# FFN-up by Strassen's scheme: seven block products in place of eight in a two-layer decoder step

## The reference

```python
def swiglu(h, w1, w3, w2):
    return (jax.nn.silu(h @ w1) * (h @ w3)) @ w2

h = rmsnorm(x, w['norm_ffn1'])
x = x + 0.5 * swiglu(h, w['ffn1_w1'], w['ffn1_w3'], w['ffn1_w2'])
...
x = x + m @ w['w_o']
h = rmsnorm(x, w['norm_ffn2'])
x = x + 0.5 * swiglu(h, w['ffn2_w1'], w['ffn2_w3'], w['ffn2_w2'])
gate = jax.nn.sigmoid(rmsnorm(x, w['norm_ple']) @ w['w_ple_gate'])
x = x + gate * (ple.astype(x.dtype) @ w['w_ple'])
```

## Time and profile before

| | |
|---|---|
| median of 3 runs | 2717.16 us (2717.04 to 2717.97) |
| span of the profiled execution | 2715.9 us (no other time of it is given) |
| TensorE busy | 2679.2 us, 99% |
| DVE, ACT, POOL busy | 1353.4, 1028.2, 241.3 us |
| matmuls | 23860 |
| read from HBM | 290.30 MB |

### The profile page before, as it was taken

How to read it: one execution, slowest core, us unless ns; L and a number is a source line. 1 busy time by engine, 2 the same in 40 slices (tenths; PEclk the granted TensorE clock), 3 DMA queues, 4 the chain that set the end, 5 groups by cost and what they waited for, 6 DMA issues and landing times.

```text
span 2715.9 us, 56484 instructions
## 1 busy us (share of the span) xinstructions
PE 2679.2 (99%) x23860; PEld 2545.4 (94%) x23860; DVE 1353.4 (50%) x1708; ACT 1028.2 (38%) x1184; POOL 241.3 (9%) x150
## 2 busy tenths in 40 slices
PE   8999999999999999999999999999999999999997
PEld 8999999976699999999999999999757999999997
DVE  5333338665666533333643333467466755333336
ACT  5333223423653433332343332333246624333223
POOL 0111000331000011100001100012310000111000
PEclk9999999999999999999999999999999999999998
DMA  4222232178422222222322222322873222222221
GB/s 149 92 93 78 96 128 95 66 239 283 146 93 94 92 90 90 84 82 90 109 94 93 92 72 94 125 93 87 282 259 120 78 94 94 93 93 78 86 100 63
DMA packets 119536, 303.81 MB, mean 112 GB/s; under 512 B 14947, under 2 KB 25187, under 8 KB 118883
## 3 DMA queue, kind: packets, MB, share of 16 engines
q1 hardware_dynamic: 119394, 301.79, 32.5%
HBM read 290.30 MB, written 11.44 MB: 111 GB/s over the span
## 4 chain that ended last, share of the span: by engine, by line
PE 94%; DVE 3%; DVEq 1%; ACT 1%; issue 0%; DMA 0%; SPq 0%; POOLq 0%; ACTq 0%
PE ps L620 70%; PE ps L668 13%; PE ps L835 2%; PE ps L927 1%; PE ps L990 1%; PE ps L975 1%; PE ps L716 1%; PE ps L946 1%; PE ps L721 1%; PE ps L1144 1%; DVEq L1819 0%; PE ps L1004 0%; DVE sc L2031 0%; PE ps L1036 0%; PE ps L1008 0%
## 5 line engine op out<-in xcount | busy, mean ns | idle before, releaser
L620 PE MATMUL ps<-Hh,whi 128*128 128x260 f32 x3440 | 692.6, 283 | 11.9 <-DVE Hl L1745 10.4
L1246 ACT ACTIVATE whi<-raw 128x2048 fp32r<-128x2048 f32 (+2 forms) x225 | 396.0, 1760 | 780.1 <-PE ps L620 670.9
L620 PE MATMUL ps<-Hl,whi 128*128 128x260 f32 x3440 | 690.7, 282 | 0.0
L620 PE MATMUL ps<-Hh,wlo 128*128 128x260 f32 x3440 | 689.7, 282 | 0.0
L1679 DVE TENSOR_TENSOR wlo<-raw,whi 128x2048 fp32r<-128x2048 f32 (+2 forms) x213 | 444.2, 2085 | 291.9 <-ACT whi L1246 291.7
L620 PEld LDWEIGHTS ps<-Hh,whi 128*128 128x128 f32 x3440 | 528.7, 188 | 13.1 <-issue 11.3
L620 PEld LDWEIGHTS ps<-Hl,whi 128*128 128x128 f32 x3440 | 530.9, 189 | 0.0
L620 PEld LDWEIGHTS ps<-Hh,wlo 128*128 128x128 f32 x3440 | 530.0, 189 | 0.0
L1246 ACT ACT_TABLE_LOAD x163 | 209.1, 1283 | 305.8 <-PE ps L620 233.5
L1679 DVE TENSOR_TENSOR ta<-ps,R 128x520 f32<-128x520 f32 x88 | 61.6, 700 | 475.9 <-PE ps L620 474.7
L620 PE MATMUL ps<-Gh,whi 128*128 128x260 f32 x1408 | 283.7, 283 | 0.0
(11 more groups left out here) (288 smaller groups left out, 2899.2 us busy)
## 6 DMA issues: line engine op xcount, KB each, us to landing
raw<-in_ffn_up SPq DMA_DIRECT2D x176, 512.0 KB, 4.3
raw<-in_ffn_down SPq DMA_DIRECT2D x128, 352.0 KB, 3.1
kb<-in_cache_k SPq DMA_DIRECT2D x128, 256.0 KB, 3.9
kb<-in_cache_v SPq DMA_DIRECT2D x128, 256.0 KB, 4.0
raw<-in_w_in SPq DMA_DIRECT2D x56, 512.0 KB, 4.4
raw<-in_w_gate SPq DMA_DIRECT2D x32, 512.0 KB, 4.5
raw<-in_w_ab SPq DMA_DIRECT2D x16, 512.0 KB, 4.3
raw<-in_w_o SPq DMA_DIRECT2D x16, 512.0 KB, 4.2
```

What stands on the lines that cost most here:

```text
L620: last = nc.tensor.matmul(ps[:, bank + 2 * m + c, 0:HT], w, x[:, k0 + k, c * HT:(c + 1) * HT], start=starts and k == 0 and n == 0, stop=st ...
L1246: return nc.scalar.activation(out, in_, func, **kw)
```

## The change

The product [X0 X1] by [w1 w3] is seen as a 2 x 2 block product: the tokens in two halves, the channels in even and odd chunks, the columns as w1 and w3. Strassen's scheme (in Winograd's form) makes it of seven products in place of eight, from sums of blocks of weights and sums of blocks of activations.

- Weights: of the four quarters of a block (512 columns each) POOL makes three more by four subtractions (`up_sums`, one of them a step on the way to another). ACT and DVE split seven quarters in three groups, UHa/ULa in two halves and UHb/ULb.
- Activations: `pair_act` and `pair_dve` take two chunks at a time: two scaled copies, four sums of 260 columns on DVE, and the split of seven parts into HA and HB. Of block 0 the first three products may run on a pair as it becomes ready, the others wait for all four pairs.
- TensorE: `up_block` runs seven products of 4 x 3 matmuls, each into one bank. Products 4 and 7 add into the bank of product 1, product 5 into that of product 2; ACT copies the bank's content out before each. DVE adds the copy to the bank when the block is done, and then multiplies by R.
- FFN-down goes over two groups of four output chunks, first half of the rows and then second half for each.
- The FFN loops of DVE, ACT, POOL and SP are written out; buffers are laid out anew; the low parts of G of the first ten blocks are made within the loop, two blocks later, the other twelve behind it.

The core of the diff (`HT` is 260; `WF` are two raw buffers, weven and wodd, and weven_71, wodd_66 in the order are their second parts):

```diff
-            def ffn(L, nb, up, down, first=0):
-                with sp_.Fori(first, KF // 2) as i:
-                    for p in range(2):
-                        load(L, nb + 2 * i + p, p, dyn(up, L, 2 * i + p))
-                with sp_.Fori(0, KD) as i:
-                    for hf in range(2):
-                        load(L, nb + KF + 2 * i + hf, hf, dyn(down, L, 2 * i + hf), cols=11 * P)
+            def ffn(L, nb, up, down, hid):
+                for n in range(KF):
+                    if n == 1:
+                        sp_.wait_ge(block_done, L * NB + nb + FREE)
+                    else:
+                        sp_.wait_ge(split_done, L * NB + nb + (n or 1) + 1)
+                    for q in range(2):
+                        sp_.dma_start(WF[n % 2][q][:, 0:3:2, :],
+                                      up[L, n][:, 1024 * q:1024 * (q + 1)].rearrange("p (a c) -> p a c", a=2)
+                                      ).then_inc(raw_ready[n % 2], 16)
+                for n in range(2 * KD):
+                    sp_.wait_ge(split_done, L * NB + nb + KF + (n if n > 1 else 0) + 1)
+                    if n == 1:
+                        sp_.wait_ge(up_sum, 4 * (up_first(L, hid) + KF) - 3)
+                    for a0 in (0, 11 * P // 2):
+                        sp_.dma_start(rawd[n % 2][:, a0:a0 + 11 * P // 2], down[L, n][:, a0:a0 + 11 * P // 2]
+                                      ).then_inc(raw_ready[n % 2], 16)
+                    if hid and n == 1:
+                        sp_.wait_ge(split_done, L * NB + nb + KF + FREE)
+                        sp_.dma_start(PT[:, :, :], A["p"][L]).then_inc(p_load, 16)
...
+            BANK = (2, 3, 1, 2, 3, 0, 2)
+
+            def up_waits(L, nb, ub, nj, hid, n, p, f):
+                g = up_first(L, hid)
+                if f == 0:
+                    pe.wait_ge(up_lo, 2 * n + (2 * g + 1))
+                    pe.wait_ge(evac, L * NE + n + (ub + 1))
+                elif f == 2:
+                    pe.wait_ge(up_lo, 2 * n + (2 * g + 2))
+                elif f == 4:
+                    pe.wait_ge(split_done, n + (L * NB + nb + FREE + 1))
+                if f in (3, 4, 6):
+                    pe.wait_ge(up_copy, 4 * n + (4 * g + {3: 1, 4: 2, 6: 3}[f]))
+
+            def up_product(p, f, i0=0, i1=4, before=None):
+                for i in range(i0, i1):
+                    if before:
+                        before(i)
+                    w = slice(i * P, (i + 1) * P)
+                    for t, (a, x) in enumerate(((WH[f], XH[f]), (WH[f], XL[f]), (WL[f], XH[f]))):
+                        last = nc.tensor.matmul(ps[:, 4 * p + BANK[f], 0:HT], a[:, w], x[:, i, :],
+                                                start=f in (0, 1, 2, 5) and i == 0 and t == 0, stop=i == 3 and t == 2,
+                                                skip_group_check=True)
+                if i1 == 4:
+                    last.then_inc(block_done if f == 6 else up_form, 1)
+
+            def up_block(L, nb, ub, nj, hid, n, p):
+                for f in range(7):
+                    up_waits(L, nb, ub, nj, hid, n, p, f)
+                    up_product(p, f)
+
+            def up_begin(L, nb, ub, nj, hid):
+                x = 4 * (2 * L + hid)
+
+                def raw_part(i):
+                    pe.wait_ge(hx_raw, x + i + 1)
+
+                def all_part(i):
+                    pe.wait_ge(hx_all, x + i + 1)
+
+                for f in range(3):
+                    up_waits(L, nb, ub, nj, hid, 0, 0, f)
+                    up_product(0, f, 0, 3, all_part if f == 1 else raw_part)
+                for f in range(3):
+                    up_product(0, f, 3, 4, all_part if f == 1 else raw_part)
+                norm_sum(L, nj)
+                for f in range(3, 7):
+                    up_waits(L, nb, ub, nj, hid, 0, 0, f)
+                    up_product(0, f)
+                pe.wait_ge(rt_ready, L * NORMS + (nj + 1))
+                up_block(L, nb, ub, nj, hid, 1, 1)
+
             def ffn(L, nb, ub, nj, hid):
-                first_pair(L, nb, ub, nj)
+                up_begin(L, nb, ub, nj, hid)
                 with pe.Fori(1, KF // 2) as i:
                     for p in range(2):
-                        block8(L, nb + 2 * i + p, ub + 2 * i + p, p, nj)
-                with pe.Fori(0, KD // 2) as i:
-                    for j in range(4):
-                        m, hf = j // 2, j % 2
-                        split_ready(L, nb + KF + 4 * i + j)
-                        if hf == 0:
-                            banks_ready(L, ub + KF + 2 * i + m)
-
-                        pe.wait_ge(gl_done, L * 2 * KF + (hid * KF + 11 * (hf + 1) + FREE))
-                        product(hf, P, 11, 1, Gh, Gl, 4 * m, starts=hf == 0, stops=hf == 1, k0=11 * hf)
+                        up_block(L, nb, ub, nj, hid, 2 * i + p, p)
+                low = L * 2 * KF + hid * KF + FREE
+
+                def eleventh(k):
+                    if k == 10:
+                        pe.wait_ge(gl_done, low + 11)
+
+                for q in range(2):
+                    for hf in range(2):
+                        for j in range(4):
+                            split_ready(L, nb + KF + 8 * q + 4 * hf + j)
+                            if hf == 0:
+                                pe.wait_ge(evac, L * NE + FREE + ub + (KF + j + 1 if q else KF - 1 + j // 2))
+                            pe.wait_ge(gl_done, low + (KF if q or hf else 10))
+                            product(j % 2, P, 11, 1, Gh, Gl, 2 * j, starts=hf == 0, stops=hf == 1, k0=11 * hf,
...
+        def pair_act(act, L, nj, hid, i):
+
+            n = 4 * (2 * L + hid) + i
+            if i:
+                act.wait_ge(hx_all, n)
+            for q in range(2):
+                nx = nc.scalar.activation(HA0[:, 4 + 2 * q:6 + 2 * q, i, :], halves(X[:, 2 * i + q, :]), ACT.Copy,
+                                          scale=gain(L, nj, 2 * i + q))
+            nx.then_inc(hx_gain, 1)
+            act.drain()
+            nc.scalar.activation(HA[:, 1:4, i, :], HA0[:, 5:8, i, :], ACT.Copy).then_inc(hx_hraw, 1)
+
+        def pair_squares(act, L, nj, hid, i):
+            act.wait_ge(acc_ready, L * NH + KD * nj + 2 * i)
+            for q in range(2):
+                nc.scalar.activation(ta[:, q, :], X[:, 2 * i + q, :], ACT.Square).then_inc(sq_ready, 1)
+
+        def pair_sums_act(act, L, nj, hid, i):
+            act.wait_ge(hx_sum, 4 * (2 * L + hid) + i + 1)
+            nc.scalar.activation(HA[:, 0, i, :], HA0[:, 4, i, :], ACT.Copy)
+            nc.scalar.activation(HB[:, 0:3, i, :], HB0[:, 3:6, i, :], ACT.Copy).then_inc(hx_hsum, 1)
...
+            dve.wait_ge(hx_gain, n)
+            V.tensor_tensor(s3, x11, s1, ALU.subtract)
+            V.tensor_tensor(s1, s1, x22, ALU.add)
+            dve.drain()
+            V.tensor_tensor(s2, s1, x11, ALU.subtract)
+            dve.drain()
+            V.tensor_tensor(s4, x12, s2, ALU.subtract).then_inc(hx_sum, 1)
+            dve.wait_ge(hx_hraw, n)
+            dve.drain()
+            V.tensor_tensor(HA[:, 5:8, i, :], HA0[:, 5:8, i, :], HA[:, 1:4, i, :].bitcast(F32), ALU.subtract
+                            ).then_inc(hx_raw, 1)
+            dve.wait_ge(hx_hsum, n)
+            dve.drain()
+            V.tensor_tensor(HA[:, 4, i, :], s1, HA[:, 0, i, :].bitcast(F32), ALU.subtract)
+            V.tensor_tensor(HB[:, 3:6, i, :], HB0[:, 3:6, i, :], HB[:, 0:3, i, :].bitcast(F32), ALU.subtract
+                            ).then_inc(hx_all, 1)
...
+                up_high(L, nb, hid, 0, 2)
+                for n in range(KF):
+                    if n:
+                        up_out(L, nb, nj, hid, n - 1, 6)
+                        up_high(L, nb, hid, n, 2)
+                    up_out(L, nb, nj, hid, n, 0)
+                    up_out(L, nb, nj, hid, n, 1)
+                    if n + 1 < KF:
+                        up_high(L, nb, hid, n + 1, 0)
+                    if n:
+                        up_silu(L, hid, n - 1)
+                    else:
+                        norm_root(L, nj)
+                    up_out(L, nb, nj, hid, n, 3)
+                    if n + 1 < KF:
+                        up_high(L, nb, hid, n + 1, 1)
+                    if 0 < n <= GE:
+                        gate_high(L, hid, n - 1)
...
+                less(1, 6, 0)
+                pool.drain()
+                if n == 1:
+                    pool.wait_ge(sum_ready, L * NORMS + 2 * hid + 1)
+                less(3, 4, 1)
+                less(6, 4, 6)
+                pool.drain()
+                less(5, 2, 3)
```

444 lines of the change are left out of this document (258 added, 186 removed).

## The result

| | before | after |
|---|---|---|
| median beside the changed kernel, 5 runs each | 2717.16 us (2716.05 to 2720.05) | 2729.30 us (2725.96 to 2731.01) |
| ratio, 95% interval | | 1.0038 [1.0027, 1.0050] |
| time and span of the profiled execution | span 2715.9 | 2725.96, span 2723.9 |
| matmuls | 23860 | 22804 |

The change makes the kernel slower by 0.3 to 0.5%, where I had forecast no change. The time lies within my range (2668 to 2762); its middle, no change, is not what came.

What follows compares the result with a forecast made beforehand. TensorE's matmuls were taken to bound the kernel; -120.4 + 60 + 7.4 + 20.9 + 17.9 + 9 + 5.4 = +0.2 on a span of 2715.9 gave 2717 us, no change. The range was 2668 to 2762.

Steps and rivals of the forecast that it cites:

- sum of holds: FFN-up blocks: POOL and DVE exclude each other, holds total 11.2 us with a Gl, 10.0 without, against TensorE's 10.04.
- Rival A: FFN blocks: holds overlap better or ACT sets the time, so no surcharge there; 2641 us; chance 0.13.
- rival B: FFN blocks: the lock couples POOL's and DVE's rows, 0.5 us more in all 88 blocks, +44, 2761 us; chance 0.25.
- -120.4: FFN-up blocks: 12 of 96 matmuls fewer, 1.434 us less in each of 21 blocks of four FFNs; ceiling for the gain.
- 2.7 of half clock: Program start and layer 1: first 28 matmuls after thin stretches run slower, 2.7 us each, +5.4 in all.
- +3.7 each: FFN start after w_o, twice: last pair's preparation and product 4 delay block 1, +7.4 us in all.
- W: After w_o: the end of w_o's last block, from which pair, product 4 and block 1 were forecast.
- my chain of a pair: FFN starts: two activation chunks pass ACT, DVE, ACT, DVE in turn, 5.7 us, and the next pair waits.
- V: Start of layer 1: the end of the gate's last product; product 4 forecast at V + 28, block 1 at V + 33.5.
- rival C: FFN-up blocks: new order of banks or weights lengthens the matmul pitch, level by 0.13 us a matmul; chance 0.02.
- Block 1's wait: Block 1 of each FFN: fifth product waits 2.2 us behind DVE's reciprocal and third split, +9 us in all.
- +60: FFN-up blocks: surcharge of the POOL-DVE lock, 15 us per FFN from ten blocks at 11.3 and ten at 10.3.

Runs made afterwards that it cites:

- e2: Changed kernel with POOL's four weight sums per block replaced by memsets of the same target that read nothing (FFN computed on other weights): 2654.62 us, ratio 0.9759.
- e1: Changed kernel with one input of the multiplications ta x R and tb x R moved from SBUF to PSUM: 2671.56 us, ratio 0.9821.
- e3: Changed kernel with POOL's subtraction for Gl replaced by three memsets in all 22 blocks of each FFN, waits kept: 2717.46 us, ratio 0.9994.
- e6: Changed kernel with the ten Gl of the loop made in every second block instead of ten blocks in a row: 2750.51 us, ratio 1.0116.
- e8: Changed kernel with each Gl of the loop made one block later on POOL, still ten in a row: 2733.58 us, ratio 1.0049.
- c1: The changed kernel once more without any edit, 7 executions and a second profile: 2728.20 us, ratio 1.0029.
- e5: Changed kernel with added matmuls of constants keeping TensorE busy in its waits at the FFN starts: 2725.41 us, ratio 1.0025.
- e9: Changed kernel with R's multiplications reading PSUM, Gl in every second block, and ACT not waiting for the previous pair's end: 2660.08 us, ratio 0.9784.

## Why the prediction was wrong

What held: the count of matmuls and the new block's pace where nothing holds it up (10.05 us for 84 in e2, where I had 10.04); the lock between POOL and DVE's two-input operations, down to the operation that TensorE waits for (ULb, before the fifth product). The Trainium skill, SBUF — State Buffer, section Who interferes with whom, frees a DVE operation with one input in SBUF; e1 agrees, 998 to 700 ns, and 58 us. The block times came out too, 11.30 and 10.35 for 11.3 and 10.3, but that is in part luck: I had them as a sum of holds, and e3, e6 and e8 show that this sum doesn't set a block. Rival A is refuted by e1 and e2, as a forecast for this kernel; rival B, 0.5 more in all 88 blocks, by the block times (10.35, not over 10.8, without a Gl), and its wait for Gh by e8.

The forecast was a difference of large terms, -120.4 and some +120. I set the two profiles side by side. The starts of block 1 in the four FFNs of the kernel after, and the first matmul behind w_o in layer 0:

```profile
49.89 0.41 PE L736 MATMUL ps<-HA,UHa 128*128 128x260 f32 x2
...
927.46 0.40 PE L736 MATMUL ps<-HA,UHa 128*128 128x260 f32 x2
...
945.72 0.28 PE L736 MATMUL ps<-HA,UHa 128*128 128x260 f32 x1
...
1396.02 0.28 PE L736 MATMUL ps<-HA,UHa 128*128 128x260 f32 x1
...
2293.37 0.28 PE L736 MATMUL ps<-HA,UHa 128*128 128x260 f32 x1
```

In the kernel before they start at 27.76, 930.40, 1368.42 and 2272.30. "Behind w_o" is the start of the first matmul that is no longer w_o's (918.03 and 2259.93 before, 927.46 and 2274.60 now), "behind the gate" the same for the PLE gate (1355.82 before, 1358.30 now).

| what the change adds, us | predicted | measured in the two profiles | difference |
|---|---|---|---|
| start of the program to block 1 | +17.9 and 2.7 of half clock | +22.1 | +1.5 |
| behind w_o to block 1, twice | +3.7 each | +5.9 and +6.4 | +4.9 |
| behind the gate to block 1 of layer 1 | +20.9 and 2.7 | +25.1 | +1.5 |
| block 1 to the start of FFN-down, four times | -120.4 + 60 + 9 = -51.4 | -13.4, -12.5, -12.3, -13.0: -51.2 | +0.2 |
| FFN-down, mixers, end | 0 | -0.3 | -0.3 |
| sum | +0.2 | +8.0 (2723.9 less 2715.9) | +7.8 |

- The step that failed is "**+3.7 each**" after w_o: it is 5.9 and 6.4, which is 4.9 of the 7.8 (a second profile, c1, has 6.5 and 6.2). The last pair and product 4 in the first of the two (DVE's row, then TensorE's):

```profile
928.08 1.30 DVE L1882 TENSOR_TENSOR X<-ps,X 128x520 f32<-128x520 f32 x2
...
933.89 1.21 DVE L1358 TENSOR_TENSOR HA<-HA,HA 128x260 fp32r<-128x260 f32 x1 [0.20 <-ACT HB L1337]
```

```profile
936.04 0.80 PE L736 MATMUL ps<-HA,UHa 128*128 128x260 f32 x2 [1.40 <-DVE HB L1359]
...
938.98 1.00 PE L736 MATMUL ps<-HB,UHa 128*128 128x260 f32 x2
```

Counted as in the prediction, W is 927.3 here. DVE adds w_o's last block 0.4 later than I had it, as two weight splits stand before it, and one subtraction of 260 columns meets POOL (1.21 for 0.43): the pair is ready at W + 8.7, not + 7.3. Product 4 starts at W + 11.7 for + 10.3. From there to block 1 it takes 6.7 for 5.8, and 7.2 in layer 1, as the first matmuls begin 0.215 apart: the granted clock is 0.50 from 936 to 939 and 0.57 to 941, and 0.50 from 2283 to 2289, where I had put nothing for half clock. So about 2.7 of the two comes before product 4 and 2.4 is the clock behind it (some of the 2.7 may be the clock too, as the last pair's matmuls and the norm sum run at 0.50; the table has 4.9 and not 5.1, as block 1 of the kernel before stands 0.1 later than I had it). e5, with the clock at 1.00 there, makes it 5.9 both times.
- Program start and layer 1: my chain of a pair was right (5.7 a pair predicted; 5.70 and 5.80 in TensorE's row above). At the program's start the pairs are 0.4 late and what follows the last is 2.7 longer: product 4 stands at 42.1 for 39. At layer 1 the first pair begins 2.4 late, behind two weight splits that waited for ACT's copies until 1360.09 and behind ACT's sigmoid: product 4 stands at V + 30.8 for V + 28. Against these 3.1 and 2.8 the half clock behind product 4 costs less than my 2.7 each: 1.5 and 1.3 less. That the two rows are off by only 1.5 each is luck.
- The gain was too high as well. A block of the kernel before takes 11.43 us and not 11.47 (DVE's evacuation of one block stands at 96.72 in the earlier trace rows, that of the next here):

```profile
108.15 0.70 DVE L1679 TENSOR_TENSOR ta<-ps,R 128x520 f32<-128x520 f32 x1 [5.11 <-PE ps L620]
```

My 0.1195 a matmul was the mean of a stretch that has FFN-down in it. The matmuls of FFN-up begin 0.1190 apart before and 0.1196 now, so the term is -116.2 and not -120.4; whether that is the one bank, as in rival C, or something else, no run shows. Block 1's wait offset it: 2.2 predicted, 0.8 to 1.3 seen, 4.2 in all for the 9. What is left for the lock in the blocks is 60.8 for the +60.
- The profiled execution (2725.96) is the shortest of its five; the median lies 3.3 above. With the span's 8.0 that gives, within 1 us, the 12 of the first set; the 7 executions of c1_same give 9 against their own runs of before.

One premise of the prediction was wrong without showing in the sum: that POOL's "order isn't tied to DVE's". POOL waits in every block for ACT's Gh or for a load, and both wait for DVE.

The other error is in the price of a change to the lock, which the kernel itself didn't test: I summed the holds. e3, e6 and e8 show pairs of blocks at 22.09, 22.25 and 22.76 where sums of holds say 20.6, 21.6 and 22.6. What DVE pays is the part of POOL's holds that falls on its two-input operations, 3.6 of 5.8 and 2.7 of 4.6 us a block in the kernel after. That POOL's row is released by DVE's in each block may be why the same places meet again and again; no run tests it, and why they are these places and not others isn't settled either.

The gain expected of twelve matmuls fewer is there in the end: with the lock relieved (e9, 2660.1) it is 59 us below the kernel before, 2.2%. What separates that from the 116 that the shorter blocks give is the starts, 57 there, for which I had some 60.

## What to carry to other kernels

Before work is moved to POOL, count on DVE how many operations read two inputs from SBUF: in that company a block that fits by busy time (7.6 and 6.4 of 10.04 us) ran at 11.3. Moving one input to PSUM was worth more (58 us) than any order of POOL's work, and reordering hurt (+21) as long as DVE's row was full, and helped (-7 to -9) once it was not. When a forecast is a small difference of large terms, each start-up chain of a few us decides the sign; write its chance accordingly.

## What was not expected of the hardware

- The cost of a POOL operation isn't its hold. Taking away ten of 50 holds of 1.16 us (e3) shortened a pair of blocks by 0.5 us, not by 2.3; taking two DVE holds of 0.54 away (e1) shortened a block by 0.9.
- The two engines fall into a steady beat: blocks of 12.07 and 10.02 in turn in e3, and of 12.39 and 10.37 in e8, from equal blocks of work. POOL's waits alternate with them (2.6 us for Gh in every second block of e3, 2.7 for a load in every second block of e8); the origin of the beat isn't shown.
- Matmuls of constants in the waits raise TensorE's granted clock in the profile (0.70 to 0.89 in 1355 to 1400) and don't shorten the span (2724.8 for 2723.9).
